# A transformer layer on one core: who turns the rotated q and k rows

## The chip, the core and the metric

One program on one core of a Trainium2 chip. The metric is device time in microseconds (us) of that core. The kernel before took 1012.53 us, the median of 3 runs (1011.42 to 1012.95).

## What is computed

A hybrid layer over 512 tokens of 1024 features, all in float32: two attention branches (a: block attention; b: attention over the 128 keys that an indexer picks), a gated merge, a mixture of 32 experts with two per token, and a gated projection. What matters here is the front of it:

```python
h = rms_norm(x, g_attn)
z = jnp.matmul(h, w_in)
qa, ka, va, qb, kb, vb, iq, ik, iw, ga, gb = jnp.split(z, offs, axis=-1)
qa, ka, qb, kb, iq = (apply_rope(heads(v), cos, sin) for v in (qa, ka, qb, kb, iq))  # 8 heads of 64
rel   = einsum('bqhd,bsd->bhqs', iq, ik) * 64 ** -0.5      # indexer, summed over heads with iw
score = einsum('bhqs,bqh->bqs', relu(rel), iw)             # causal, then the 128 largest of a row
o_a   = softmax(qa @ ka.T / 8, causal) @ va
o_b   = softmax(qb @ kb.T / 8, only the picked keys) @ vb
```

(The last lines are the reference's functions in short form. With 512 tokens the block attention's selection takes in every earlier block, so that branch a is causal attention.)

## The kernel before

Tokens lie on the 128 partitions, in four tiles of 128 (NT = 4). The matrix products `z = h @ w_in` give each of qa, ka, va, qb, kb, vb and iq as four PSUM tiles of 128 tokens by 512 columns. Weights come as **halves** of 1 MB (`HALVES`, numbered n), through a ring of four raw buffers: SP issues load n when VectorE has finished the low part of half n - 3 (`load`, L610). ScalarE rounds a half to its high part (`split_high`, L562), VectorE subtracts that from the raw weight (`split_low`, L569), and TensorE takes three products a pair (`three`, L744). Both splits run two halves ahead of the product. A half costs TensorE 48 matmuls.

ScalarE copies the finished tiles of iq, qa, ka, qb and kb, scaled, into one of two halves of `z_chunks` (`STAGE`: iq, qa, qb share one, ix, ka, kb the other), and GpSimd rotates them there in place (`rope`, L2138). A score needs q and k with the head's features on the partitions, so every rotated array has to be turned: 16 blocks of 128 by 128. In the kernel before TensorE turns them (`transposes`, L732), four to a PSUM bank, and ScalarE copies the bank to `iqt`, `qt` or `kt` (L1330): 20 groups, 80 turns and 20 copies. The next array that wants the same half of `z_chunks` waits until the groups of the one before are filled (L1342).

The order of the front is one list, `front_steps` (L118), and every engine walks it. Of weight to the change:

- `iq` is turned beside the first half of qa (`BESIDE_QA`, L219), and the eight `rel` of the second token tile, the first readers of `iqt`, are laid between the tiles of the second half of qa (`BESIDE_Z`). The `rel` of the third and fourth tile lie beside the two halves of ka.
- qa is turned behind the last `rel`, ka behind the first half of qb; VectorE runs 14 of the 16 rounds of the top-k (`topk_round`, three to a half) from the first half of qb on.
- qb and kb are turned inside the last four steps of attention a (`between` in `attention_steps`, L102), because they go to the same `qt` and `kt` that attention a reads.
- An attention is a pipeline of 16 units, (pair of heads, token tile): `scores` on TensorE (L935), scale, mask and maximum on VectorE (L1678), exponent on ScalarE (L1314), reciprocal of the sum on VectorE (L1763), the scaling of the rows on GpSimd (L2159), `turn_p` on TensorE (L947), a copy by ScalarE or VectorE, `pv` on TensorE (L962). Between attention a and b lie the two halves of vb, and the first scores of b stand between these.

Behind the front, the experts' weights (192 loads of 1 MB) go through 16 slots, most of which are regions that the front has used; SP issues each when TensorE is done with what the slot held.

Of the kernel before, what the change touches and what calls it, by code (L numbers as in the profile page):

```python
# [160 lines left out]
def place_banks():  # L161

    where, uses = {}, [0] * 8
    turns = rels = outs = 0
    for s in FRONT:
        kind = s[0]
        if kind in ("rope", "topk", "select", "merge"):
            continue
# [21 lines left out]
        elif kind == "turn" and s[1] in ("qb", "kb"):  # L190
            b = s[2] % 4
        elif kind == "turn":
            b = 4 + turns % 2
            turns += 1
# [7 lines left out]
        else:  # L202
# [102 lines left out]
def layer_kernel(nc, x, p, g_attn, w_in, w_br_a, w_br_b, w_out, g_ffn, w_grp, b_grp, w_rt, b_rt,  # L305
# [49 lines left out]
    qt = sb("qt", "qk", [P, NT, S])[:]  # L355
    kt_ = sb("kt", "qk", [P, NT, S], skip=8 * K)[:]
# [3 lines left out]
    iqt = sb("iqt", "o", [P, NT, S], skip=8 * K)[:]  # L360
# [82 lines left out]
    def turn_dst(s):  # L443
# [12 lines left out]
    def c4(name, k):  # L456
# [31 lines left out]
    ssq_done, ms_done, rms_done = (sem(n) for n in ("ssq_done", "ms_done", "rms_done"))  # L488
# [5 lines left out]
    x_squared, x_rooted, x_inv = sem("x_squared"), sem("x_rooted"), sem("x_inv")  # L494
# [110 lines left out]
    def _(sp):  # L605
# [125 lines left out]
    def _(pe):  # L731
# [140 lines left out]
        def front_step(s):  # L872
            kind, a, i = s
            if kind in ("rope", "topk", "select", "merge"):
# [40 lines left out]
            elif kind == "rel":  # L915
                t, h = a, i
                if (t, h) == (1, 0):
                    for cc in range(NT):
                        drained(pe, ("turn", "iq", cc))
# [3 lines left out]
                pe.matmul(ps[:, 0:(t + 1) * P], iqt[lo:lo + HD, h // 2, t * P:(t + 1) * P],  # L923
                          ikt[lo:lo + HD, 0:(t + 1) * P], start=True, stop=True
                          ).then_inc(bank_filled[BANK[s][0]], 1)
            elif kind == "scores":
                pair, t = unit(i)
                if i == 0:
                    for cc in range(NT):
                        drained(pe, ("turn", "q" + a, cc))  # L930
                        drained(pe, ("turn", "k" + a, cc))
                ps = [claim(pe, s + (h,)) for h in range(2)]
                for h in range(2):
                    lo = HD * h
                    pe.matmul(ps[h][:, 0:(t + 1) * P], qt[lo:lo + HD, pair, t * P:(t + 1) * P],  # L935
                              kt_[lo:lo + HD, pair, 0:(t + 1) * P], start=True, stop=True
# [352 lines left out]
    def _(act):  # L1289
        def square_x():  # L1290
# [971 lines left out]
```

## Time and profile before

The profiled execution took 1012.0 us, its span from first to last instruction is 1010.1 us, and the mean granted clock of TensorE 0.995. It lies inside the three runs (1011.42 to 1012.95).

| engine | busy us | share of the span |
|---|---|---|
| TensorE matmul | 974.6 | 96% |
| TensorE weight load | 601.6 | 60% |
| VectorE | 382.4 | 38% |
| ScalarE | 311.5 | 31% |
| GpSimd | 144.3 | 14% |

The chain that ended last is 80% TensorE and 12% DMA; of the latter nearly all (11%) is the load of the experts' `up` weights. The shares of VectorE, ScalarE and GpSimd are means over stages: the front (up to about 330 us here) holds most of the work of VectorE and GpSimd, so a stretch has to be read by itself.

### The profile page before, as it was taken

To read this page: it belongs to the slowest core of one execution; us is meant where nothing else is said; L and a number is where in the kernel's file an instruction comes from. 1 tells how busy PE (TensorE), PEld (TensorE's weight loads), DVE (VectorE), ACT (ScalarE), POOL (GpSimd) and SP (SyncE) were. 2 spreads that over 40 slices of the span, in tenths; PEclk is the share of its full clock that TensorE was granted. 3 is DMA by queue.
4 is the path that set the end of the run, shared out by engine and by line. 5 is a ranking of instruction groups with operands and counts; after the bars stand their busy time and mean duration, and the time that the engine had idled before them with its cause. 6 is when DMAs were issued, how large, how long until landed. Compare 5 with 4: busy or idle time off the path is not lost.

```text
span 1010.1 us, 12215 instructions
## 1 busy us (share of the span) xinstructions
PE 974.6 (96%) x4872; PEld 601.6 (60%) x4872; DVE 382.4 (38%) x788; ACT 311.5 (31%) x542; POOL 144.3 (14%) x141
## 2 busy tenths in 40 slices
PE   8999999999999999999999999999988998999896
PEld 6776887686788888885443444444433443343686
DVE  4344896655353436226121111111101111023875
ACT  6444334746442224242111111111110111211665
POOL 0320134926500000000000100000000000001300
PEclk9999999999999999999999999999999999999999
DMA  9512220000072350856999999999999999999701
GB/s 334 175 50 76 84 85 7 2 1 2 1 292 84 111 181 1 333 201 261 414 395 422 420 421 420 420 421 420 421 422 420 421 421 416 420 420 375 287 21 64
DMA packets 59146, 256.07 MB, mean 254 GB/s; under 512 B 12222, under 2 KB 12862, under 8 KB 34000
## 3 DMA queue, kind: packets, MB, share of 16 engines
q1 hardware_dynamic: 50224, 248.26, 61.5%
q0 software_dynamic: 2560, 4.20, 1.1%
q10 hardware_dynamic: 6304, 2.80, 1.0%
q8 instruction: 40, 0.66, 0.3%
q14 instruction: 18, 0.15, 0.0%
HBM read 248.95 MB, written 10.49 MB: 257 GB/s over the span
## 4 chain that ended last, share of the span: by engine, by line
PE 80%; DMA 12%; DVE 4%; POOL 2%; ACT 2%; issue 1%; SPq 1%; DVEq 0%
PE psum L747 37%; PE psum L1117 17%; DMA slot<-in_w_up 11%; PE psum L1073 5%; PE psum L1137 4%; PE psum L1138 4%; PE psum L1155 1%; PE psum L1093 1%; PE psum L1083 1%; PE psum L962 1%; PE psum L947 1%; DVE ple_gate_lo L1969 1%; PE psum L935 1%; PE psum L923 1%; POOL raw L2159 1%; PE psum L735 1%
## 5 line engine op out<-in xcount | busy, mean ns | idle before, releaser
L1117 PE MATMUL psum<-slot,xt 128*64 128x512 f32 x512 | 234.4, 601 | 11.6 <-DMA slot<-in_w_up 11.0
L1118 PE MATMUL psum<-slot,xt 128*64 128x512 f32 x512 | 234.7, 601 | 0.0
L1117 PEld LDWEIGHTS psum<-slot,xt 128*64 128x64 f32 x512 | 66.0, 137 | 134.6 <-issue 130.4
L2175 POOL DMA_INDIRECT pair_rows<-y,slot_pair x30 | 31.2, 1040 | 621.0 <-ACT y L1483 621.0
L1137 PE MATMUL psum<-slot,ht 128*64 128x512 f32 x256 | 115.9, 595 | 1.2 <-DVE ht L1993 1.2
L1138 PE MATMUL psum<-slot,ht 128*64 128x512 f32 x256 | 115.9, 595 | 0.0
L747 PE MATMUL psum<-w_hi,act_hi 128*128 128x512 f32 x288 | 115.4, 401 | 0.3 <-DVE act_lo L1629 0.3
L747 PE MATMUL psum<-w_lo,act_hi 128*128 128x512 f32 x288 | 112.5, 391 | 0.0
L747 PE MATMUL psum<-w_hi,act_lo 128*128 128x512 f32 x288 | 112.1, 389 | 0.0
L1476 ACT ACTIVATE small<-psum,slot_inv 64x512 f32<-64x512 f32 x32 | 21.9, 684 | 253.2 <-PE psum L1118 252.1
L572 DVE TENSOR_TENSOR w_lo<-raw,w_hi 128x2048 fp32r<-128x2048 f32 (+1 forms) x30 | 68.2, 2274 | 83.7 <-ACT w_hi L567 83.6
L567 ACT CAST w_hi<-raw 128x2048 fp32r<-128x2048 f32 (+1 forms) x30 | 55.9, 1865 | 72.1 <-PE psum L747 66.1
L1986 DVE SCALAR_TENSOR_TENSOR small<-psum,slot_inv,small 64x512 f32<-64x512 f32 x32 | 23.8, 744 | 129.2 <-ACT small L1476 129.2
L1993 DVE COPY ht<-psum 128x256 f32<-128x256 f32 x32 | 13.6, 424 | 145.3 <-PE psum L1093 142.8
L1118 PEld LDWEIGHTS psum<-slot,xt 128*64 128x64 f32 x512 | 65.9, 137 | 0.0
L747 PEld LDWEIGHTS psum<-w_hi,act_hi 128*128 128x128 f32 x288 | 54.1, 188 | 17.2 <-issue 5.9
L747 PEld LDWEIGHTS psum<-w_lo,act_hi 128*128 128x128 f32 x288 | 54.1, 188 | 11.7
L747 PEld LDWEIGHTS psum<-w_hi,act_lo 128*128 128x128 f32 x288 | 54.2, 188 | 10.4
L1942 DVE TENSOR_TENSOR xt<-psum,g_by_place 128x512 f32<-128x512 f32 x32 | 20.7, 687 | 103.1 <-PE psum L1083 103.1
L1138 PEld LDWEIGHTS psum<-slot,ht 128*64 128x64 f32 x256 | 33.7, 137 | 36.5 <-issue 36.5
L1137 PEld LDWEIGHTS psum<-slot,ht 128*64 128x64 f32 x256 | 33.7, 137 | 34.2 <-issue 32.9
L747 PE MATMUL psum<-act_hi,w_hi 128*128 128x512 f32 (+1 forms) x136 | 53.5, 394 | 0.0
(292 smaller groups left out, 1528.3 us busy)
## 6 DMA issues: line engine op xcount, KB each, us to landing
slot<-in_w_gate SPq DMA_DIRECT2D x64, 1024.0 KB, 20.7
slot<-in_w_up SPq DMA_DIRECT2D x64, 1024.0 KB, 22.2
slot<-in_w_down SPq DMA_DIRECT2D x64, 1024.0 KB, 22.2
raw<-in_w_in SPq DMA_DIRECT2D x21, 1024.0 KB, 5.0
raw<-in_w_out SPq DMA_DIRECT2D x4, 1024.0 KB, 5.4
pair_in<-pair_rows SPq DMA_DIRECT2D x4, 1024.0 KB, 14.3
slot<-in_w_ple_gate SPq DMA_DIRECT2D x4, 1024.0 KB, 8.3
rows_tok<-in_x SPq DMA_DIRECT2D x8, 256.0 KB, 5.4
```

Of the source, the lines that this page charges most:

```text
L567: act.copy(w_hi_at[n][:, 0:w], raw_at[n][:, 0:w]).then_inc(hi_done, 1)
L572: dve.tensor_tensor(w_lo_at[n][:, 0:w], raw_at[n][:, 0:w], w_hi_at[n][:, 0:w].bitcast(F32), ALU.subtract).then_inc(lo_done, 1)
L747: mms = [pe.matmul(ps, a, b, start=first and n == 0, stop=last and n == 2) for n, (a, b) in enumerate(ops)]
L1073: mm = pe.matmul(bank[(1, 7)[h]], pick[:, t, :], by_chunk(part[:, t], h), start=part is x1_hi and t == 0, stop=part is x1_lo and t == NT - 1)
L1117: mm_g = pe.matmul(ps[FIRST:2 * FIRST, :], left, g[:, k, :], start=first, stop=last)
L1118: mm_u = pe.matmul(ps[0:FIRST, :], left, u[:, k, :], start=first, stop=last)
L1137: pe.matmul(ps[0:FIRST, :], left, w[:, k, 0:512], start=first, stop=last)
L1138: mm = pe.matmul(ps[FIRST:2 * FIRST, :], left, w[:, k, 512:1024], start=first, stop=last)
L1476: act.activation(small[0:FIRST, 0, :], bank[2 + e % 2][FIRST:2 * FIRST, :], ACT.Silu, scale=slot_inv[FIRST:2 * FIRST, e:e + 1]).then_inc(s ...
L1942: dve.tensor_tensor(xt[:, q % 2, 4 * g:4 * g + 4, :], bank[g].rearrange("p (k s) -> p k s", k=4), g_by_place[:, 4 * g:4 * g + 4].unsqueeze ...
L1986: dve.scalar_tensor_tensor(out=small[0:FIRST, 1, :], in0=bank[2 + e % 2][0:FIRST, :], scalar=slot_inv[0:FIRST, e:e + 1], in1=small[0:FIRST ...
L2175: pool.indirect_dma_start(out=pairs_d.rearrange("r (h d) -> (r h) d", h=2), out_offset=bass.IndirectOffsetOnAxis(ap=index, axis=0), in_=y, ...
```

## The change

VectorE turns each 128 by 512 tile of `z_chunks` in place, in blocks of 32 by 32 (new step `flip`, four instructions for an array). Within a block rows and columns are then exchanged, but the blocks themselves still stand where they stood. SP moves these: for each pair of a source quarter and a destination quarter of the partitions one DMA, 16 DMAs for an array (`flip_blocks`), each of 32 partitions by 16 blocks by 32 elements, so 512 pieces of 128 bytes and 64 KB. For this `iqt`, `qt` and `kt` are laid out by token tile first. The 80 turns on TensorE and the 20 copies on ScalarE are gone. The readers wait on a new semaphore `flipped`.

Where SP issues them is set by a table, behind the loads n = 9, 12, 14 and 16. Some semaphores are merged, to make room for the two new ones; the instructions around them stay.

```diff
-def attention_steps(branch, between=()):
+def attention_steps(branch):
...
-        if u >= NU - 1:
-            out += between[:2]
-            between = between[2:]
...
+    flip = lambda name: [("flip", name, 0)]
-    st += z("qa")[:1] + [("ix_back", 0, 0), ("rope", "ix", 0)] + turn("iq", NT) + turn("ix", 1)
+    st += z("qa")[:1] + [("ix_back", 0, 0), ("rope", "ix", 0)] + flip("iq") + turn("ix", 1)
...
-    st += z("ka")[:1] + rel(2) + z("ka")[1:] + rel(3) + [("rope", "ka", 0)] + turn("qa", NT)
+    st += z("ka")[:1] + rel(2) + flip("qa") + z("ka")[1:] + rel(3) + [("rope", "ka", 0)]
...
-        if n == 0:
-            st += turn("ka", NT)
+        st += {0: flip("ka"), 3: flip("qb"), 4: flip("kb")}.get(n, [])
...
-    st += [("scores", "a", 2)] + attention_steps("a", turn("qb", NT) + turn("kb", NT))
+    st += [("scores", "a", 2)] + attention_steps("a")
...
-BESIDE_QA = {0: [("ix_back", 0, 0)], 1: [("turn", "iq", 0), ("turn", "iq", 1)], 2: [("turn", "iq", 2), ("turn", "iq", 3)],
-             3: [("turn", "ix", 0)]}
+BESIDE_QA = {0: [("ix_back", 0, 0)], 1: [], 2: [], 3: [("turn", "ix", 0)]}
+FLIPS = ["iq", "qa", "ka", "qb", "kb"]
+FLIP_BEHIND_LOAD = {9: ["iq"], 12: ["qa"], 14: ["ka"], 16: ["qb", "kb"]}
+QUARTER = P // 4
...
+    def flip_done(eng, name):
+
+        eng.wait_ge(flipped, 16 * 16 * (FLIPS.index(name) + 1))
...
+        def flip_blocks(name):
+
+            n = FLIPS.index(name)
+            sp.wait_ge(flip_ready, n + 1)
+            if n and name != "kb":
+                sp.wait_ge(flipped, 16 * 16 * n)
+            if name == "qb":
+                for h in range(2):
+                    filled(sp, ("scores", "a", NU - 1, h))
+            dst = {"iq": iqt, "qa": qt, "qb": qt, "ka": kt_, "kb": kt_}[name]
+            z = stage_z[:, STAGE[name]].rearrange("p t (c b j) -> p (t c) b j", b=4, j=QUARTER)
+            to = dst.rearrange("p t c (a j) -> p (t c) a j", a=4, j=QUARTER)
+            for a in range(4):
+                for b in range(4):
+                    sp.dma_start(to[QUARTER * b:QUARTER * b + QUARTER, :, a, :], z[QUARTER * a:QUARTER * a + QUARTER, :, b, :]
+                                 ).then_inc(flipped, 16)
...
+            for name in FLIP_BEHIND_LOAD.get(n, []):
+                flip_blocks(name)
...
                 if (t, h) == (1, 0):
-                    for cc in range(NT):
-                        drained(pe, ("turn", "iq", cc))
+                    flip_done(pe, "iq")
                     drained(pe, ("turn", "ix", 0))
...
                 if i == 0:
-                    for cc in range(NT):
-                        drained(pe, ("turn", "q" + a, cc))
-                        drained(pe, ("turn", "k" + a, cc))
+                    flip_done(pe, "k" + a)
...
                     prev = ROPES[ROPES.index(a) - 2]
-                    for cc in range(1 if prev == "ix" else NT):
-                        filled(act, ("turn", prev, cc))
+                    if prev == "ix":
+                        filled(act, ("turn", prev, 0))
+                    else:
+                        flip_done(act, prev)
...
+            if kind == "flip":
+                dve.wait_ge(roped, ROPES.index(a) + 1)
+                z = stage_z[:, STAGE[a]]
+                for t in range(NT):
+                    ins = dve.transpose(z[:, t], z[:, t])
+                ins.then_inc(flip_ready, 1)
+                return
```

The order of instructions on SP, from load n = 2 on. `raw` is the ring of weight halves, `x6` six instructions in a row of that form.

```order
L617 DMA raw<-in_w_in 128x8x72 [waits front_loaded_2]
L617 DMA raw<-in_w_in 128x4x512 [waits front_loaded_3]
L617 DMA raw<-in_w_in 128x4x512 [waits lo_done] x13
L617 DMA raw<-in_w_br_a 128x4x512 [waits bank_filled_7,lo_done]
L617 DMA raw<-in_w_in 128x4x512 [waits bank_filled_7,lo_done]
```

That was the kernel before: loads n = 2, 3, the thirteen from 4 to 16, and the next two. The changed kernel, from behind load n = 9:

```order
L645 DMA iqt<-z_chunks 32x16x32 [waits flip_ready]
L645 DMA iqt<-z_chunks 32x16x32 x15
L615 DMA raw<-in_w_in 128x4x512 [waits lo_done] x3
L645 DMA qt<-z_chunks 32x16x32 [waits flipped,flip_ready]
L645 DMA qt<-z_chunks 32x16x32 x15
L615 DMA raw<-in_w_in 128x4x512 [waits lo_done] x2
L645 DMA kt<-z_chunks 32x16x32 [waits flipped,flip_ready]
L645 DMA kt<-z_chunks 32x16x32 x15
L615 DMA raw<-in_w_in 128x4x512 [waits lo_done] x2
L645 DMA qt<-z_chunks 32x16x32 [waits bank_filled_2,bank_filled_3,flipped,flip_ready]
L645 DMA qt<-z_chunks 32x16x32 x15
L645 DMA kt<-z_chunks 32x16x32 [waits flip_ready]
```

Eighty DMAs now stand among the loads; those of qb and kb wait for the last scores of attention a (`bank_filled_2` and `bank_filled_3`), and the loads behind them stand behind that wait.

On TensorE, the last half of qa up to its first `rel` (L923 before, L939 now): before

```order
L747 MATMUL psum<-w_hi,act_hi 128x512
L747 MATMUL psum<-w_hi,act_lo 128x512
L747 MATMUL psum<-w_lo,act_hi 128x512
L923 MATMUL psum<-ikt,iqt 128x256 [waits bank_drained_5,bank_drained_4,bank_drained_6]
L923 MATMUL psum<-ikt,iqt 128x256 [waits bank_drained_7]
```

and now

```order
L764 MATMUL psum<-w_hi,act_hi 128x512
L764 MATMUL psum<-w_hi,act_lo 128x512
L764 MATMUL psum<-w_lo,act_hi 128x512
L939 MATMUL psum<-ikt,iqt 128x256 [waits bank_drained_6,bank_drained_4,flipped]
L939 MATMUL psum<-ikt,iqt 128x256 [waits bank_drained_7]
```

The place is the same; the 16 turns of iq, eight of them 36 and eight 24 weight matmuls ahead of it, are gone, and the first `rel` waits for the DMAs instead of ScalarE's copies.

On VectorE, between the third and the fourth top-k round (L1772 and L1775 before, L1795 and L1798 now): before

```order
L1775 MATCH_REPLACE work<-m_137,work 128x384 [waits max_done]
L1775 MATCH_REPLACE work<-m_137,work 128x512 [waits max_done]
L572 TENSOR_TENSOR w_lo<-raw,w_hi 128x2048 [waits hi_done]
L1772 MAX m_137<-work 128x8 [waits mark_done] x3
L1775 MATCH_REPLACE work<-m_137,work 128x256 [waits max_done]
```

and now

```order
L1798 MATCH_REPLACE work<-m_137,work 128x384 [waits max_done]
L1798 MATCH_REPLACE work<-m_137,work 128x512 [waits max_done]
L1639 STREAM_TRANSPOSE z_chunks<-z_chunks 128x512 [waits roped]
L1639 STREAM_TRANSPOSE z_chunks<-z_chunks 128x512 x3
L570 TENSOR_TENSOR w_lo<-raw,w_hi 128x2048 [waits hi_done]
L1795 MAX m_137<-work 128x8 [waits mark_done] x3
```

The four block turns of ka stand ahead of the low part of the next half; those of qb and kb stand in the same way behind the twelfth and the fourteenth round.

## Rows read from the trace of the kernel before

**Rows 1.** Windows: us, busy (x) of PE, PEld, DVE, ACT, POOL, clock, DMA share, GB/s.
```profile
140.00:155.00 15.00, 15.00 (x68) 12.42 (x67) 15.00 (x33) 5.84 (x6) 5.23 (x5) 1.00 0.36 82
...
180.00:200.00 20.00, 18.97 (x170) 11.74 (x168) 13.27 (x51) 14.17 (x44) 18.90 (x18) 1.00 0.01 2
```

**Rows 2.** Timeline of PE near 46: start us, us, engine, operation [idle before <-releaser].
```profile
46.55 1.03 PE L735 MATMUL psum<-cst,z_chunks 128*128 128x128 f32 x8
...
47.34 0.47 PE L747 MATMUL psum<-w_hi,act_hi 128*128 128x512 f32 x1
...
57.12 0.70 PE L923 MATMUL psum<-ikt,iqt 64*128 64x256 f32 x4
```

**Rows 3.** Timeline of DVE near 46.
```profile
46.25 0.18 DVE L1655 SCALAR_TENSOR_TENSOR iws<-psum,inv_x 128x32 f32<-128x32 f32 x1
56.91 2.29 DVE L572 TENSOR_TENSOR w_lo<-raw,w_hi 128x2048 fp32r<-128x2048 f32 x1 [10.47 <-ACT w_hi L567]
```

**Rows 4.** Timeline of DVE inside the top-k rounds.
```profile
125.88 0.68 DVE L1775 MATCH_REPLACE8 work<-m,work 128x512 f32<-128x512 f32 x1
126.48 1.47 DVE L1772 MAX8 m<-work 128x8 f32<-128x256 f32 x3
```

**Rows 5.** Timeline of SP, back-to-back issues, from its second row on.
```profile
4.98 2.14 SPq L635 DMA_DIRECT2D rows_tok<-in_x  x4
```

**Rows 6.** DMA issues: KB each, median us from issue to landing.
```profile
cst<-constants SPq DMA_DIRECT2D x1, 64.0 KB, 2.0
```

**Rows 7.** Instructions of tile wr: ns of one (min, median, max).
```profile
L1401 ACTq DMA_DIRECT2D wr<-in_w_rt x1: 604/604/604, 150.2 to 150.2; - x1
```

**Rows 8.** DMA queue of ACT, 150 to 155: packets, MB, share of 16 engines.
```profile
q10 hardware_dynamic: 3536, 0.17, 44.3%
```

**Rows 9.** Timeline of DVE, from the last rel to the third score tile.
```profile
100.58 2.40 DVE L1670 SCALAR_TENSOR_TENSOR work<-small,iws,work 128x512 f32<-128x512 f32 x2 [2.42 <-ACT small L1372]
...
105.18 2.29 DVE L572 TENSOR_TENSOR w_lo<-raw,w_hi 128x2048 fp32r<-128x2048 f32 x1 [2.20 <-ACT w_hi L567]
...
118.34 2.29 DVE L572 TENSOR_TENSOR w_lo<-raw,w_hi 128x2048 fp32r<-128x2048 f32 x1 [1.98 <-ACT w_hi L567]
...
160.65 0.67 DVE L1678 CUSTOM_DVE_ANT_0 small<-psum,cst 128x512 f32<-128x512 f32 x1
...
165.50 2.29 DVE L572 TENSOR_TENSOR w_lo<-raw,w_hi 128x2048 fp32r<-128x2048 f32 x1 [2.41 <-ACT w_hi L567]
...
172.72 0.56 DVE L1678 CUSTOM_DVE_ANT_0 small<-psum,cst 128x384 f32<-128x384 f32 x1 [4.93 <-PE psum L935]
```

**Rows 10.** Timeline of POOL in the first attention.
```profile
173.93 3.62 POOL L2159 TENSOR_SCALAR small<-small,rs 128x128 f32<-128x128 f32 x4 [7.63 <-DVE rs L1763]
...
204.10 1.82 POOL L2159 TENSOR_SCALAR small<-small,rs 128x256 f32<-128x256 f32 x2
```

**Rows 11.** Timeline of PE: its last scores of a, and what follows.
```profile
199.41 0.70 PE L935 MATMUL psum<-kt,qt 64*128 64x256 f32 x4
...
209.36 0.66 PE L962 MATMUL psum<-gain,v 128*64 128x128 f32 x8
...
209.95 0.50 PE L747 MATMUL psum<-w_hi,act_hi 128*128 128x512 f32 x1
...
221.05 1.35 PE L935 MATMUL psum<-kt,qt 64*128 64x512 f32 x8
```

**Rows 12.** Timeline of PE: two of its longest waits.
```profile
780.04 0.61 PE L1117 MATMUL psum<-slot,xt 128*64 128x512 f32 x1 [2.47 <-DMA slot<-in_w_up]
...
958.97 0.76 PE L747 MATMUL psum<-ple_gate_hi,tail_hi 128*128 128x512 f32 x1 [3.76 <-DVE ple_gate_lo L1969]
```

**Rows 13.** Windows of two us behind the first of them.
```profile
780.00:782.00 2.00, 1.96 (x8) 0.87 (x10) 0.00 (x0) 0.00 (x0) 0.00 (x0) 0.72 1.03 430
782.00:784.00 2.00, 2.00 (x8) 0.72 (x6) 0.00 (x0) 0.00 (x0) 0.00 (x0) 0.50 0.97 406
```

**Rows 14.** Waits of SP: engine, line, for whom: us in total, times, longest.
```profile
SPq L698 <- PE psum L1118: 164.8, 55, 14.5
```

More of the change, by code:

```diff
@@ L99, in unit @@
     return u // NT, (3, 0, 2, 1)[u % NT]
-def attention_steps(branch, between=()):
-    out, between = [], list(between)
+def attention_steps(branch):
+    out = []
     for u in range(LAG, NU + LAG + 1):
@@ L111, in attention_steps @@
             out.append(("pv", branch, u - LAG - 1))
-        if u >= NU - 1:
-            out += between[:2]
-            between = between[2:]
-    assert not between
     return out
@@ L163, in place_banks @@
     where, uses = {}, [0] * 8
-    turns = rels = outs = 0
+    rels = 0
     for s in FRONT:
         kind = s[0]
-        if kind in ("rope", "topk", "select", "merge"):
+        if kind in ("rope", "topk", "select", "merge", "flip"):
             continue
@@ L189, in place_banks @@
             b = s[2] % 4
-        elif kind == "turn" and s[1] in ("qb", "kb"):
-            b = s[2] % 4
         elif kind == "turn":
-            b = 4 + turns % 2
-            turns += 1
+            b = 4
         elif kind == "rel":
@@ L354, in layer_kernel @@
     act_lo = sb("act_lo", "lo", [P, KD, S], F32R)
-    qt = sb("qt", "qk", [P, NT, S])[:]
-    kt_ = sb("kt", "qk", [P, NT, S], skip=8 * K)[:]
+    qt = sb("qt", "qk", [P, NT, NT, P])[:]
+    kt_ = sb("kt", "qk", [P, NT, NT, P], skip=8 * K)[:]
     v_sb = sb("v", "v", [P, NT, AW])[:]
@@ L475, in layer_kernel @@
     picked, x_gathered, x_copied, halves_made = sem("picked"), sem("x_gathered"), sem("x_copied"), sem("halves_made")
-    (tail_turned, tail_high, tail_low, tail_filled, tail_gated, tail_squared, tail_rms, tail_inv, added, last_squared,
+    (tail_turned, tail_high, tail_low, tail_filled, tail_gated, tail_squared, tail_inv, added, last_squared,
      last_ms, last_rms, last_out) = (sem(n) for n in (
-         "tail_turned", "tail_high", "tail_low", "tail_filled", "tail_gated", "tail_squared", "tail_rms", "tail_inv",
+         "tail_turned", "tail_high", "tail_low", "tail_filled", "tail_gated", "tail_squared", "tail_inv",
          "added", "last_squared", "last_ms", "last_rms", "last_out"))
@@ L487, in layer_kernel @@
     x1_turned, x1t_copied, x1t_last = sem("x1_turned"), sem("x1t_copied"), sem("x1t_last")
-    ssq_done, ms_done, rms_done = (sem(n) for n in ("ssq_done", "ms_done", "rms_done"))
+    ssq_done, ms_done, rooted = (sem(n) for n in ("ssq_done", "ms_done", "rooted"))
     logits_done, slots_spread, slots_listed = (sem(n) for n in ("logits_done", "slots_spread", "slots_listed"))
@@ L513, in layer_kernel @@
     first_turned, first_low = sem("first_turned"), sem("first_low")
+    flip_ready, flipped = sem("flip_ready"), sem("flipped")
     def claim(pe, step):
@@ L873, in front_step @@
             kind, a, i = s
-            if kind in ("rope", "topk", "select", "merge"):
+            if kind in ("rope", "topk", "select", "merge", "flip"):
                 return
@@ L934, in front_step @@
                     lo = HD * h
-                    pe.matmul(ps[h][:, 0:(t + 1) * P], qt[lo:lo + HD, pair, t * P:(t + 1) * P],
-                              kt_[lo:lo + HD, pair, 0:(t + 1) * P], start=True, stop=True
+                    pe.matmul(ps[h][:, 0:(t + 1) * P].rearrange("p (t s) -> p t s", s=P), qt[lo:lo + HD, t, pair, :],
+                              kt_[lo:lo + HD, 0:t + 1, pair, :], start=True, stop=True
                               ).then_inc(bank_filled[BANK[s + (h,)][0]], 1)
@@ L1812, in route @@
             link(dve.tensor_scalar(v, ms, 1.0 / D, EPS, ALU.mult, ALU.add))
-            dve.wait_ge(rms_done, 1)
+            dve.wait_ge(rooted, 2)
             link(dve.reciprocal(y, sq))
@@ L2099, in tail_inverse @@
             dve.wait_ge(tail_squared, t + 2)
-            inverse(*(stat[:, 4 * k + t:4 * k + t + 2] for k in range(5)), inv_tail[:, t:t + 2], (tail_rms, t // 2 + 1), tail_inv)
+            inverse(*(stat[:, 4 * k + t:4 * k + t + 2] for k in range(5)), inv_tail[:, t:t + 2], (rooted, t // 2 + 3), tail_inv)
         dve.wait_ge(proj_done, 2 * NT)
```

16 lines of the change are left out of this document (7 added, 9 removed).

## The prediction, made before the changed kernel ran

> **What bounds the kernel now.** I read the windows by stage first, then the timelines of TensorE and VectorE at each turn that goes, then what waits for what in attention a. TensorE is busy nearly throughout, and a shift of it in the front counts in full later: the experts' loads wait for TensorE to finish with a slot (55 of them for 164.8 us in all, [rows 14]), so they start earlier or later with the front, and the end moves with them. But two stretches have a second bound. From 140 to 155 VectorE is busy 15.00 of 15.00 us, and from 180 to 200 GpSimd 18.90 of 20 [rows 1]. The reader is to see that taking work from TensorE is worth its full price only outside these.
>
> **What goes.** 20 groups of four turns. A pair of groups costs TensorE 0.79 us (46.55 to 47.34, [rows 2]), ten pairs some 8 us, a little more with the waits for ScalarE's copies between groups. By itself that would be the gain. The 20 copies on ScalarE go too.
>
> **The turn of iq.** Before, the first `rel` starts at 57.12 [rows 2]; two pairs less bring TensorE there at 57.12 - 1.6 = 55.5. What it now waits for: VectorE is free at 46.25 + 0.18 = 46.4 and idle for the next 10.47 us [rows 3], so its four block turns are hidden there. Their price the trace does not show. The nearest is the pass of 512 columns that is followed after 0.60 us (125.88 to 126.48, [rows 4]); I take 0.60 each, 2.4 us an array, with bounds of half and twice that. Ready at about 48.9. Then SP issues 16 DMAs. Four of 256 KB in a row take SP 2.14 us, 0.53 each [rows 5]; ScalarE's issue of 1024 small pieces took 0.60 [rows 7]; a DMA of 64 KB lands 2.0 us after its issue [rows 6]. With 0.53 the last is issued at 48.9 + 15 x 0.53 = 56.9 and lands at 58.9. The pieces are only 128 bytes. 3536 small ones took 44.3% of 16 engines over 5 us, 35.4 us, that is 10.0 ns each [rows 8]; 512 per engine make 5.1 us an array, below the 8.5 us of the issues, so I let the issue set the pace. Low end 0.32 us a DMA (5.1 / 16), high end 2.0 us (no DMA overlaps the next).
>
> So `rel` starts at 58.9 and not 57.12: plus 1.7, and TensorE has stood idle 3.3 us. In the kernel before, a wait of 3.76 us was one of its longest, and one of 2.47 us [rows 12] was followed by a granted clock of 0.72 and 0.50 over four us, so partly at 1.2 instead of 2.4 GHz: 2 x 0.28 + 2 x 0.50 = 1.6 us of full-speed work lost [rows 13]. 3.3 lies above that wait, and I count the fall: plus 1.6. Behind the wait on SP stand the loads from n = 10 on; the low part of half 10 is made at 118.34 only [rows 9]. ScalarE's first copy of qa waits for the same DMAs, beside TensorE.
>
> The Trainium skill, TensorE: Matmul & The Clock Gate, section HAM oscillation, describes just this: DMA waits between matmuls drop the clock and the next matmuls run cold. The trace agrees, with 0.50 behind the wait of 2.47 us.
>
> All later times leave out this shift of 3.3 against the kernel before; it is added at the end.
>
> **VectorE until attention a.** The turn of qa lies in front of the low part of a half that is wanted two halves later, and costs nothing. From the last `rel` on VectorE is the clock. Before, it ends these at 100.58 + 2.40 = 102.98 and then waits 2.20 us for ScalarE, which is still copying turned qa; now it goes on at 102.98: minus 2.2. The turn of ka adds 2.4, of which 1.98 us fills the wait at 118.34: the chain now stands at minus 2.2 + 2.4 - 2.0 = -1.8. The turns of qb and kb add 4.8: the scores of a, begun at 160.65, begin at 163.7. TensorE is there over 3 us earlier than before (four pairs at 0.79 for qa and ka, and the waits between them) and does the second half of va meanwhile. Behind the scores stand ScalarE's exponents and cast and then the low part at 165.50 + 3.0 = 168.5, which ends at 170.8. Before, VectorE was idle 4.93 us here, for TensorE, until 172.72 [rows 9]; now TensorE is early and 170.8 decides. GpSimd, the busiest engine of attention a, restarts at 173.93 - 1.9 = 172.0 [rows 10]. Of TensorE's gain 1.9 us is left there.
>
> **The tail of attention a.** GpSimd works without a gap until 204.10 + 1.82 = 205.9, now 204.0 [rows 10]. Before, TensorE still had turns of kb to do and began vb at 209.95. Now only the last turns (0.4, half a pair), one copy (about 0.7) and the last `pv` (0.66, [rows 11]) stand behind GpSimd: 1.8 us, so vb begins at 205.8: 4.1 or 4.2 early.
>
> **The turns of qb and kb.** SP issues 32 DMAs once the last scores of a are made: 199.41 + 0.70 - 1.9 = 198.2. Last issue 31 x 0.53 = 16.4 later, landed at 216.6. The scores of b are wanted at 205.8 + (221.05 - 209.95) = 216.9 [rows 11]. Hidden, with 0.3 us to spare: from 0.54 us a DMA on, each further 0.01 us costs 0.3. No load is held up: the next one waited until the end of attention b before.
>
> **Sum.** -4.2 (start of vb) + 1.7 (iq late) + 1.6 (clock) + 0 (kb) = -0.9 us. Against the profiled 1012.0 that is 1011.1; the median of the runs is 0.5 higher: 1012.53 - 0.9 = 1011.6.
>
> **Rivals.** *Short wait.* With 0.43 us a DMA the iq blocks land at 48.9 + 6.5 + 2.0 = 57.4, plus 0.2 instead of 1.7, TensorE is idle 1.9 us and the clock holds: -4.2 + 0.2 = -4.0, 1008.6. For it: the pieces of the last DMA alone need 0.32 us, and [rows 13] stands behind a longer wait. Against: 0.53 is the measured pace of back-to-back issues, and load 9 is in flight at the same time.
>
> *Slow pieces (slower).* If a piece from one partition quarter to another costs an engine 20 ns instead of 10.0, a DMA takes 32 x 20 = 0.64 us and the pieces set the pace. iq lands at 48.9 + 9.6 + 2.0 = 60.5, plus 3.4, with the clock 5.0; qb and kb land at 198.2 + 19.8 + 2.0 = 220.0, 3.1 behind the need: -4.2 + 5.0 + 3.1 = +3.9, 1016.4. At 1 us a DMA it would be +8.8 + 1.6 + 14.3 - 4.2 = +20.5. It decides from about 0.56 us a DMA on. For it: each DMA reads only 32 partitions and writes only 32, which no row shows; [rows 8] reads memory and writes all 128. Against: only the rate of [rows 8].
>
> The Trainium skill speaks on both sides. DMA: Bandwidth & Descriptors, section Specifications, wants 512 bytes for line rate and says that shorter ones are read, modified and written; by that this rival holds. The same page, section Why small descriptors are slow (HBM only), exempts transfers between SBUF and SBUF; by that the sum above holds. No run so far shows such a transfer.
>
> *Dear block turns.* At twice the price, iq is 2.4 later and the chain into attention a 7.2: -0.9 + 9.6 = +8.7, 1021.2; at half, minus 1.2 and minus up to 3.6: 1006.8. Nothing in the trace speaks for either.
>
> *Full price.* If VectorE is not what attention a waits for, all eight pairs behind iq count: -6.3 + 3.3 = -3.0, 1009.5. Against it stands the full window of VectorE in [rows 1].
>
> **Chances.** Forecast 0.35, its own range 1009.6 to 1013.2; short wait 0.26; slow pieces 0.27; dear (or cheap) turns 0.08; full price 0.04. The range is 1007.5 to 1021: it takes in both rivals and leaves out the far ends. A difference below 0.2%, 2.0 us, can hardly be told from none here. Faster by more: 0.07 of the forecast, 0.24 of the short wait, 0.06 of the last two, 0.37. Slower by more: 0.25 of the slow pieces, 0.05 of dear turns, 0.02 of the forecast, 0.32. The rest, 0.31, is the same.
>
> **What the next profile shows.** Block turns of 0.6 us starting at about 46.4. SP's 16 issues in 8.5 us and the last landing near 58.9; an idle stretch of TensorE of 3.3 us in front of the first `rel` (L939) and a clock under 1.00 behind it. VectorE's first score tile of a about 3 us later than 160.65 plus the shift, GpSimd's restart 1.9 us earlier than 173.93 plus the shift, vb begun at 205.8 plus the shift. No wait for DMAs in front of the first scores of b. A long wait there makes the prediction wrong towards slower; no idle time in front of the first `rel` makes it wrong towards faster.

## The result and the profile after

The changed kernel takes 1020.67 us (median of 4 runs, 1019.63 to 1021.6) against 1012.11 us (4 runs) of the kernel before: ratio 1.0084, 95% interval 1.0066 to 1.0101. It is slower by 8.6 us. The prediction said 1011.6, no change or slightly faster; the time lies just inside its range, close to the upper end. The profiled span is 1019.6 us against 1010.1, so the trace has 9.5 us to explain. Executions of one kernel scatter by 2 to 3 us, so a difference of less than about 1 us between two medians says little here.

Two new waits for DMAs stand in it. First TensorE, in the timeline around the first `rel` (start us, us, engine, operation, idle time before and what ended it):

```profile
55.27 0.39 PE L764 MATMUL psum<-w_lo,act_hi 128*128 128x512 f32 x1
61.76 1.23 PE L939 MATMUL psum<-ikt,iqt 64*128 64x256 f32 x4 [6.11 <-DMA iqt<-z_chunks]
```

TensorE is ready at 55.65, where the prediction had it, and stands still for 6.11 us. The `rel` that began at 57.12 [rows 2] begins at 61.76: plus 4.64, not 1.7. On VectorE the block turns of iq lie in the idle time of [rows 3], each four of them 2.4 to 2.5 us:

```profile
46.66 2.48 DVE L1639 STREAM_TRANSPOSE z_chunks<-z_chunks 128x512 f32<-128x512 f32 x4
55.35 2.29 DVE L570 TENSOR_TENSOR w_lo<-raw,w_hi 128x2048 fp32r<-128x2048 f32 x1 [6.21 <-ACT w_hi L565]
```

So the pieces start on time. What is late is the row of issues on SP (timeline of SP; the row's duration covers all its issues):

```profile
49.16 10.85 SPq L645 DMA_DIRECT2D iqt<-z_chunks  x16
...
204.45 11.76 SPq L645 DMA_DIRECT2D qt<-z_chunks  x16
216.25 10.74 SPq L645 DMA_DIRECT2D kt<-z_chunks  x16
```

and, one by one, ns of an issue (min, median, max), first and last start in us:

```profile
L645 SPq DMA_DIRECT2D qt<-z_chunks x32: 597/632/1723, 96.9 to 215.6; - x32
L645 SPq DMA_DIRECT2D kt<-z_chunks x32: 590/631/1612, 125.8 to 226.4; - x32
L645 SPq DMA_DIRECT2D iqt<-z_chunks x16: 617/631/755, 49.2 to 59.4; - x16
```

Sixteen take 10.85 us where [rows 5] let me expect 8.5; from start to start that is (59.4 - 49.2) / 15 = 0.68 us. (The longest of an issue, 1.6 to 1.7 us, fall in the sets of qa, ka and qb.) The granted clock behind both waits (windows of 2 us, columns as in [rows 1]):

```profile
60.00:62.00 2.00, 0.24 (x2) 0.24 (x4) 0.00 (x0) 0.26 (x1) 0.00 (x0) 0.50 0.74 92
62.00:64.00 2.00, 2.00 (x7) 1.16 (x8) 0.48 (x1) 1.09 (x3) 0.00 (x0) 0.50 0.94 314
64.00:66.00 2.00, 2.00 (x8) 1.62 (x7) 0.48 (x1) 0.00 (x0) 0.00 (x0) 0.74 0.47 183
228.00:230.00 2.00, 1.30 (x4) 0.79 (x6) 0.00 (x0) 0.00 (x0) 0.00 (x0) 0.50 0.11 15
230.00:232.00 2.00, 2.00 (x8) 1.17 (x7) 1.08 (x3) 0.35 (x1) 0.00 (x0) 0.50 0.00 0
232.00:234.00 2.00, 2.00 (x9) 1.61 (x9) 0.82 (x7) 2.00 (x9) 0.54 (x1) 0.93 0.03 8
```

A clock of 0.50 is 1.2 GHz instead of 2.4. From 61.76 to 66 it costs 2.24 x 0.50 + 2 x 0.26 = 1.6 us; behind the second wait, from 228.70, 3.3 x 0.50 and 0.1 in the next window, 1.8 us. VectorE, the answer to [rows 9]:

```profile
106.69 2.44 DVE L1693 SCALAR_TENSOR_TENSOR work<-small,iws,work 128x512 f32<-128x512 f32 x2 [2.41 <-ACT small L1388]
109.05 2.82 DVE L570 TENSOR_TENSOR w_lo<-raw,w_hi 128x2048 fp32r<-128x2048 f32 x1
...
123.08 2.24 DVE L570 TENSOR_TENSOR w_lo<-raw,w_hi 128x2048 fp32r<-128x2048 f32 x1
...
169.20 0.66 DVE L1701 CUSTOM_DVE_ANT_0 small<-psum,cst 128x512 f32<-128x512 f32 x1
...
176.25 0.55 DVE L1701 CUSTOM_DVE_ANT_0 small<-psum,cst 128x384 f32<-128x384 f32 x1
```

Against [rows 9], VectorE's part of the last `rel` is 6.1 late; the wait of 2.20 us behind it is gone (109.05 is only 3.9 late); the wait at 118.34 has been filled by the turn of ka; the scores of a are 8.5 late; and at 176.25 VectorE comes without idle time, where it idled 4.93 us before. That is the chain of the prediction, step by step; the sizes are compared further below. GpSimd [rows 10] and TensorE [rows 11]:

```profile
177.45 3.63 POOL L2182 TENSOR_SCALAR small<-small,rs 128x128 f32<-128x128 f32 x4 [2.60 <-DVE rs L1786]
...
208.30 1.83 POOL L2182 TENSOR_SCALAR small<-small,rs 128x256 f32<-128x256 f32 x2
```

```profile
211.31 0.66 PE L976 MATMUL psum<-gain,v 128*64 128x128 f32 x8
...
228.70 2.50 PE L949 MATMUL psum<-kt,qt 64*128 64x512 f32 x8 [5.61 <-DMA kt<-z_chunks]
```

The last product of attention a was over at about 210.0 and is over at 211.97; the scores of b are wanted at 228.70 - 5.61 = 223.09 and start at 228.70. From measured times alone: the scores of b are wanted 2.04 later than in the kernel before (223.09 against 221.05), wait 5.61 and lose 1.8 to the clock, together +9.45; the spans differ by 9.5. The 2.04 are the lateness of iq and its clock, 4.64 + 1.6, less 4.2 gained in between, which is the prediction's own step for vb (-4.1 or -4.2).

### The profile page after: what moved, and what is told of

The parts are those of the page before. It is cut to its first block, busy times and chain, and to the rows that moved or that the text cites. A ratio compares the mean times of both kernels' runs of the same rounds, so it can differ in the third digit from the quotient of the medians.

```text
span 1019.6 us, 12121 instructions
## 1 busy us (share of the span) xinstructions
PE 970.3 (95%) x4792; PEld 596.6 (59%) x4792; DVE 394.3 (39%) x808; ACT 301.0 (30%) x522; POOL 142.5 (14%) x141
## 4 chain that ended last, share of the span: by engine, by line
PE 70%; DMA 12%; DVE 10%; SPq 3%; ACT 2%; issue 1%; POOL 1%; DVEq 0%
PE psum L764 28%; PE psum L1131 17%; DMA slot<-in_w_up 11%; PE psum L1087 5%; PE psum L1151 4%; PE psum L1152 4%; SPq L645 3%; DVE work L1798 2%; DVE m L1795 2%; PE psum L1107 1%; PE psum L1169 1%; DVE w_lo L570 1%; PE psum L1097 1%; PE psum L949 1%; PE psum L976 1%
## 5 line engine op out<-in xcount | busy, mean ns | idle before, releaser
L1131 PE MATMUL psum<-slot,xt 128*64 128x512 f32 x512 | 232.7, 597 | 12.4 <-DMA slot<-in_w_up 11.8
L764 PEld LDWEIGHTS psum<-w_lo,act_hi 128*128 128x128 f32 x288 | 54.6, 190 | 11.8
```

The source lines that it names most:

```text
L764: mms = [pe.matmul(ps, a, b, start=first and n == 0, stop=last and n == 2) for n, (a, b) in enumerate(ops)]
L1131: mm_g = pe.matmul(ps[FIRST:2 * FIRST, :], left, g[:, k, :], start=first, stop=last)
```

## The experiments

Two theories on the pace. *Issue theory*: a DMA costs its issuing engine some 0.7 us, whatever it carries. *Piece theory*: the 16 DMA engines are held up by 128-byte pieces. Independently of both, each wait should have a price of its own. "Before" is timed in the same calls (medians 1011.87 to 1012.09).

One caution on times of day in different traces. Four of the kernels below have the same steps as the kernel before up to the first `rel`, and no DMA wait there; it starts at 57.14, 56.77, 57.59 and 55.88, and at 57.12 in the kernel before. So a later time is best counted from the first `rel` of its own trace, or the scatter of the start is taken for an effect.

**One wait removed: iq on TensorE again.**

```
-    st += ... + flip("iq") + turn("ix", 1)
+    st += ... + turn("iq", NT) + turn("ix", 1)
-BESIDE_QA = {..., 1: [], 2: [], ...}
+BESIDE_QA = {..., 1: [("turn", "iq", 0), ("turn", "iq", 1)], 2: [("turn", "iq", 2), ("turn", "iq", 3)], ...}
```

> One part undone: iq is turned by TensorE again, the other four arrays as in the changed kernel. If each DMA wait costs what stands late behind it (my theory: two separate prices, 6.1 us for iq and 7.3 for qb and kb), 6.1 comes back: 1020.7 - 6.1 = 1014.6 us, no idle stretch in front of the first rel, and still 5 to 6 us idle in front of the first scores of b. Rival (the waits hide one another, since the later one only absorbs the lateness of the first): the wait in front of the scores of b grows by what iq gave back, and the time stays near 1020.7.

Measured 1014.99 us (6 runs), ratio to before 1.0033 (1.0021 to 1.0046): 5.7 us came back of the expected 6.1. `rel` begins at 57.14 without a wait, and the wait for kb is still there:

```profile
222.85 2.50 PE L954 MATMUL psum<-kt,qt 64*128 64x512 f32 x8 [5.23 <-DMA kt<-z_chunks]
```

The rival falls: the waits don't hide one another, since SP starts the second set of DMAs behind the scores of a and so is earlier by what TensorE is.

**The other wait removed: qb and kb in two halves.** The order of a staged array is changed to head pair, token tile, column, so that a half is one run of pieces (the edit in short form):

```
+for half in range(2):
+    sp.wait_ge(flipped, ...)                         # what was issued before has landed
+    filled(sp, ("scores", "a", (NU // 2 if half == 0 else NU) - 1, h))
+    ... 32 DMAs: dst[:, 2 * half:2 * half + 2] <- z[:, 2 * half:2 * half + 2]
-scores of b, step 0: wait for kb
+scores of b, step 0: wait for the first half; step 2: wait for the second
```

> iq as in the changed kernel. qb and kb go in two halves (head pairs 0 and 1, then 2 and 3), 32 DMAs of 256 pieces each; the first half as soon as attention a has made its scores of pair 1, the second behind the last scores of a; the third scores step of b waits for the second half. Issue theory (a DMA costs SP some 0.72 us whatever its size): 23 us a half, the first lands near 210, the second near 230, before TensorE wants it near 234; no idle in front of the scores of b, 1020.7 - 7.3 = 1013.4 us. Piece theory (the pace is that of the pieces): a half takes 11.5 us, the time is the same 1013.4, but SP's pitch is about 0.36 us. So the time tests the price of the wait, and the pitch tells the two theories apart.

Measured 1014.47 us (5 runs), 1.0029 (1.0016 to 1.0043). TensorE goes into the scores of b at 224.46 without a wait, so the price of this wait is confirmed in form; 6.2 us came back of the expected 7.3. In the profiled execution the clock stayed low longer behind a wait for iq of the same length (TensorE, then windows):

```profile
61.33 1.22 PE L954 MATMUL psum<-ikt,iqt 64*128 64x256 f32 x4 [6.09 <-DMA iqt<-z_chunks]
```
```profile
64.00:66.00 2.00, 2.00 (x6) 1.58 (x5) 0.07 (x1) 0.00 (x0) 0.00 (x0) 0.50 0.21 82
66.00:68.00 2.00, 2.00 (x7) 1.27 (x7) 0.00 (x0) 0.17 (x1) 0.00 (x0) 0.64 0.00 0
```

The clock is 0.50 from 60 to 66 there: 4.67 x 0.50 + 2 x 0.36 = 3.1 us lost and not 1.6. The pace of SP, one by one:

```profile
L643 SPq DMA_DIRECT2D qt<-z_chunks x32: 585/611/1269, 187.6 to 221.6; - x32
```

256 pieces take 611 ns to issue, 512 took 631: the pace does not follow the pieces. This is the first blow to the piece theory.

**Both waits removed.** The two edits together.

> Both of the above: iq on TensorE, qa and ka as in the changed kernel, qb and kb in halves. By the sum of the prediction without its two DMA waits the start of vb is 4.2 us earlier than before and nothing waits behind it: 1012.1 - 4.2 = 1007.9 us; the two prices read from the trace of the changed kernel give 1020.7 - 6.1 - 7.3 = 1007.3. Rival (VectorE, which makes the block turns, is the bound and gives nothing back): 1012.1, no faster than before.

Measured 1007.86 us (5 runs), ratio 0.9963 (0.9949 to 0.9978): faster than the kernel before. Attention a's last product ends at 206.1 against 210.0, 3.9 early, or 3.6 counted from the first `rel` (56.77 against 57.12), where 4.2 were predicted; nothing is lost behind it. GpSimd, then TensorE:

```profile
170.98 3.62 POOL L2205 TENSOR_SCALAR small<-small,rs 128x128 f32<-128x128 f32 x4 [2.61 <-DVE rs L1809]
...
202.42 1.82 POOL L2205 TENSOR_SCALAR small<-small,rs 128x256 f32<-128x256 f32 x2
```
```profile
205.43 0.66 PE L998 MATMUL psum<-gain,v 128*64 128x128 f32 x8
217.13 1.35 PE L971 MATMUL psum<-kt,qt 64*128 64x512 f32 x8
```

**Two queues for iq.** Half of the 16 DMAs are issued by ScalarE:

```
-                for b in range(4):
+                for b in range(0, 4, 2 if name == "iq" else 1):      # SP; ScalarE issues b = 1 and 3
```

> Only who issues the 16 DMAs of iq is changed: 8 from SP and 8 from ScalarE. Issue theory: 8 x 0.72 us on either side, the last issue near 54 and landed near 56.5, TensorE idle below 1 us and no fall of the clock: 1020.7 - 6.1 = 1014.6 us. Piece theory (16 engines work off the pieces at the measured pace): the blocks land near 61.7 as before, 1020.7 us.

Measured 1019.79 us (4 runs), 1.0080 (1.0065 to 1.0095). The time is what the piece theory expected; but the timeline of ScalarE shows that the trial was badly built. Its eight issues stand behind its copy of ix, start at 53.12 and end at 58.8, when SP has been done since 54.85. `rel` waits until 60.48. It tells nothing apart, so I moved them:

```
+            if s == ("flip", "iq", 0):
+                act.wait_ge(flip_ready, 1)           # in front of the copy of ix
```

> As the previous kernel with two queues, but ScalarE issues its 8 DMAs of iq as soon as the block turns are made (near 49) instead of behind its copy of ix (53.1). Issue theory: both queues at 0.7 us a DMA side by side, last issue near 54.6, landed near 57, rel there and not at 61.8, TensorE idle about 1.3 us, clock held: 1020.7 - 4.7 - 1.5 = 1014.5 us. Piece theory: side by side each queue falls to about 1.4 us a DMA, rel stays near 61.7, 1020.7 us.

Measured 1019.23 us (4 runs), 1.0071 (1.0049 to 1.0093). Now both queues run at once (timelines of SP, ScalarE and TensorE):

```profile
48.19 6.75 SPq L645 DMA_DIRECT2D iqt<-z_chunks  x8
```
```profile
48.19 6.85 ACTq L1341 DMA_DIRECT2D iqt<-z_chunks  x8
```
```profile
58.00 0.70 PE L939 MATMUL psum<-ikt,iqt 64*128 64x256 f32 x4 [3.33 <-DMA iqt<-z_chunks]
```

Sixteen in 6.85 us and not in 10.85: the wait falls from 6.11 to 3.33. Neither theory had its number. Two queues do share the work, so SP's issuing was what set the pace; but side by side an issue takes 0.84 to 0.86 us, and landing 3.5 to 3.7 us instead of 2.3, so a second bound stands close behind, and this run doesn't say which. The Trainium skill, DMA: Bandwidth & Descriptors, section Issuing engines are not separate DMA queues, says that a second issuing engine saves only issue time, "which is usually small relative to the DMA itself". The first half agrees with the trace. The second fits one of these DMAs (issued in 0.63 us, landed in 2.3) but not the set: 16 issues one behind the other take 10.85 us, most of the time until the last has landed. I had expected 6.2 us back and got 1.4 by the median of four runs (1017.39 to 1020.21). The trace explains about 2.2: the wait for iq is 2.8 shorter and the one for kb 0.55 longer (6.16), and the clock fell all the same, though only after TensorE had resumed at 58.00:

```profile
58.00:60.00 2.00, 2.00 (x9) 1.44 (x10) 2.00 (x2) 1.33 (x3) 0.00 (x0) 0.87 0.00 0
60.00:62.00 2.00, 2.00 (x7) 1.51 (x6) 0.67 (x2) 0.00 (x0) 0.00 (x0) 0.50 0.53 87
```

**TensorE kept busy in the wait for iq.**

```
+                    for _ in range(24):
+                        pe.matmul(ps, act_hi[:, 0, 0:P], act_hi[:, 1, :], start=True, stop=True)
                     flip_done(pe, "iq")
```

> The changed kernel; in front of its wait for the blocks of iq TensorE makes 24 products of act_hi with itself (128x512, about 5.5 us), whose result nobody reads. The wait stays. If the granted clock of 0.62 to 0.68 behind the wait is what idling costs: clock 1.00 behind it, 1.5 us less up to the last rel, 1020.7 - 1.5 = 1019.2 us. Rival (the clock falls for another reason, or the time is lost in the DMA wait alone): no change.

Measured 1019.12 us (6 runs), 1.0067 (1.0049 to 1.0084), about 1.5 us less than the changed kernel, though the intervals of the two overlap. The trace is clearer: idle time 0.67 us, and no fall:

```profile
61.19 0.70 PE L943 MATMUL psum<-ikt,iqt 64*128 64x256 f32 x4 [0.67 <-DMA iqt<-z_chunks]
```
```profile
62.00:64.00 2.00, 2.00 (x10) 1.62 (x11) 0.97 (x2) 0.58 (x2) 0.00 (x0) 1.00 1.01 386
```

**The pace by size of the pieces.** Other data, same bytes and same count (the blocks land in wrong places, so the total time means nothing here; the edit in short form):

```
+if name in ("iq", "kb"):   to4[32 rows, :, a, :] <- z4[32 rows, :, b, :]      # 128 pieces of 512 bytes
+if name == "qa":           dst[:, a, b, :] <- z4[:, a, b, :]                   # 128 partitions, 512 bytes each
```

> A measurement of SP's pace by form, each DMA of 64 KB; the blocks land in wrong places, so this is for the issue times and not for the total. iq and kb: 32 partitions, 128 pieces of 512 bytes in place of 512 of 128. qa: all 128 partitions, one piece of 512 bytes each. ka and qb as in the changed kernel (512 pieces of 128 bytes). Issue theory: all five near 0.7 us a DMA, rel near 61.8. Piece theory: 0.7 us for ka and qb, clearly below (0.2 to 0.5) for the long pieces, and rel earlier by 15 times the difference.

One run, read only for the issues (ns of one, min, median, max):

```profile
L654 SPq DMA_DIRECT2D qt<-z_chunks x16: 550/602/735, 96.9 to 106.8; - x16
```
```profile
L647 SPq DMA_DIRECT2D iqt<-z_chunks x16: 588/601/755, 48.4 to 58.2; - x16
```

A quarter of the pieces at four times the length takes 0.601 us where the short ones took 0.631, and 128 partitions instead of 32 the same. Landing goes from 2.3 to 2.0 us. The piece theory falls as an explanation of the 16 DMAs on one queue. The rule of the Trainium skill that the prediction had on its own side (DMA: Bandwidth & Descriptors, section Why small descriptors are slow (HBM only): transfers within SBUF are exempt) agrees with this run, where short pieces cost 0.03 us an issue and 0.3 us of landing.

**The pace by source.** But why 0.63 and not the 0.53 of [rows 5]? Those rows read HBM.

```
+if name == "iq":   to[32 rows, :, a, :] <- w_in[32 rows, 0:2048] as (n b j), [:, :, b, :]     # 512 pieces, from HBM
+if name == "qa":   dst[:, a, b, :] <- w_in rows, 128 columns                                 # 128 pieces, from HBM
```

> A measurement of SP's pace by source; the blocks hold other data, so this is for the issue times and not for the total. iq: 16 DMAs with the shape of the change (32 partitions, 512 pieces of 128 bytes) but from w_in in HBM. qa: 16 DMAs of 64 KB, 128 partitions, one piece of 512 bytes each, from HBM. ka, qb, kb as in the changed kernel. If reading from SBUF is what makes an issue dear: 0.5 us a DMA for iq and qa, as for the loads of x, and 0.7 for ka. If it is the write into SBUF or the mere DMA of 64 KB: 0.65 to 0.7 for all.

One run, again for the issues:

```profile
L653 SPq DMA_DIRECT2D iqt<-in_w_in x16: 337/488/494, 48.8 to 56.6; - x16
L653 SPq DMA_DIRECT2D kt<-z_chunks x16: 627/631/642, 213.9 to 224.0; - x16
```
```profile
L648 SPq DMA_DIRECT2D qt<-in_w_in x16: 427/432/655, 95.3 to 102.7; - x16
```

The very shape of the change, read from HBM, goes at (56.6 - 48.8) / 15 = 0.52 us a DMA, the 0.53 of the prediction; read from SBUF, kb in the same run goes at (224.0 - 213.9) / 15 = 0.67, and iq in the changed kernel at 0.68. With 128 partitions and 512-byte pieces it is (102.7 - 95.3) / 15 = 0.49 from HBM against 0.66 from SBUF in the run by size of the pieces. The dear thing is an issue whose source is SBUF. (The landing goes the other way: 2.7 us for iq from HBM, 2.3 from SBUF.) Why an issue costs more stays open.

**Twelve DMAs instead of sixteen.** The blocks that stay in their own quarter of the partitions, four DMAs of the 16, are not moved by DMA. For iq VectorE copies them; for qb and kb they are left out, so that attention b computes with old blocks there.

```
+                    if a == b and name not in ("qa", "ka"):
+                        continue
+# iq only: four copies on VectorE, iqt[own, :, :, own] <- z[own][..., own]
```

> 12 DMAs instead of 16 for iq, qb and kb: the blocks on the diagonal don't go by DMA. Those of iq are copied by the idle VectorE; those of qb and kb are left out (they hold the blocks of qa and ka). At the measured 0.72 us a DMA twelve take about what sixteen take at the 0.53 of the prediction, so this puts the prediction's own numbers to the test: iq lands at 49 + 11 x 0.72 + 2.3 = 59.2, TensorE idle 3.5 us, the clock falls and costs 1.5; vb begins at 209.95 - 4.2 + 3.5 = 209.3; qb and kb land at 201.8 + 23 x 0.72 + 2.3 = 220.7 against a need of 220.4: 1011.9 - 4.2 + 3.5 + 0.3 = 1011.5 us. If the price of a DMA wait isn't what its lateness says: clearly above, toward 1020.

Measured 1009.92 us (10 runs), 0.9977 (0.9965 to 0.9989). The issues of an array now take 8.2 us, nearly the 8.5 of the prediction, and the trace is nearly the one predicted: `rel` at 58.23, idle 3.36 (predicted 58.9 and 3.3), no wait in front of the scores of b.

```profile
58.23 0.70 PE L942 MATMUL psum<-ikt,iqt 64*128 64x256 f32 x4 [3.36 <-DMA iqt<-z_chunks]
...
217.98 1.35 PE L952 MATMUL psum<-kt,qt 64*128 64x512 f32 x8
```

What does not come behind the wait for iq is the fall of the clock:

```profile
60.00:62.00 2.00, 2.00 (x11) 1.39 (x11) 0.46 (x1) 0.07 (x1) 0.00 (x0) 1.00 0.75 284
```

It held at 2.4 GHz behind 3.36 us of idling, while in the run with two queues it fell to 1.2 behind 3.33 us, and in [rows 12, 13] behind 2.47. That fits the time, 1.6 below the expected 1011.5. But this is one execution, and the clock is not always so kind in it: behind a later wait, for an expert's `up` weights, it falls.

```profile
832.59 1.09 PE L1134 MATMUL psum<-slot,xt 128*64 128x512 f32 x1 [3.14 <-DMA slot<-in_w_up]
```
```profile
834.00:836.00 2.00, 2.00 (x6) 0.53 (x4) 0.00 (x0) 0.00 (x0) 0.00 (x0) 0.50 1.00 414
```

Eight of the traces have such a wait between 830 and 844: the clock fell behind 2.44, 2.81, 3.12 and twice 3.14 us and held behind 1.79, 2.25 and 2.69. The edits do not touch that stretch. It is a likely part of the scatter of 2 to 3 us, though no run shows how much.

**Only qa and ka.** iq, qb and kb are turned by TensorE.

```
-        st += {0: flip("ka"), 3: flip("qb"), 4: flip("kb")}.get(n, [])
+        st += {0: flip("ka")}.get(n, [])
-    ... attention_steps("a")
+    ... attention_steps("a", turn("qb", NT) + turn("kb", NT))
```

> Only qa and ka are turned in the new way; iq, qb and kb are turned by TensorE as before. This asks who bounds the way into attention a. If VectorE does (the prediction): its 4.8 us of block turns for qb and kb go, so attention a starts where TensorE's four pairs less let it, 3.2 us before the kernel before and not 2.9 as in the kernel with both waits removed (about the same), but the eight pairs of turns stand behind attention a again: vb starts about 4.1 us behind GpSimd's end instead of 1.8, so at 209.95 - 3.1 = 206.9 and the time is 1012.0 - 3.1 = 1008.9 us. Rival (TensorE's work is worth its full price everywhere): four of eight pairs are given back, half of the gain of 4.0 us is left, 1010.0 us.

Measured 1007.39 us (5 runs), 0.9954 (0.9940 to 0.9967), the fastest of all, if not clearly faster than the 1007.86 of both waits removed. GpSimd restarts at

```profile
169.52 3.62 POOL L2199 TENSOR_SCALAR small<-small,rs 128x128 f32<-128x128 f32 x4 [5.10 <-DVE rs L1803]
```

4.4 us before [rows 10] and 1.5 before the 170.98 of the kernel with both waits removed (counted from the first `rel`, here at 57.59: 4.9 and 2.3), and attention a ends as much earlier than before, with the turns of qb and kb behind it. The rival's 1010.0 falls; my 1008.9 was a little high, since TensorE, which decides here, makes its third score step at 167.35 and not at 171.77: the four pairs were worth 4.4 us (4.9 from the first `rel`), with the waits between them, and not 3.2. That TensorE decides is seen on VectorE:

```profile
168.30 0.56 DVE L1718 CUSTOM_DVE_ANT_0 small<-psum,cst 128x384 f32<-128x384 f32 x1 [2.40 <-PE psum L965]
```

**More work on VectorE.** The kernel with both waits removed, with eight more block turns:

```
+                if a in ("qb", "kb"):
+                    for t in range(NT):
+                        dve.transpose(iqt[:, t], z[:, t])
```

> The kernel with both waits removed, with eight more block turns on VectorE (four beside those of qb, four beside those of kb, into a buffer that is free then), 4.8 us of work that nobody reads. If VectorE is what attention a waits for, as the prediction has it: GpSimd's restart and the start of vb come 4.8 us later, 1007.9 + 4.8 = 1012.7 us. Rival (VectorE has slack there, TensorE decides): no change, 1007.9.

Measured 1012.14 us (10 runs), 0.9996 (0.9986 to 1.0005), 4.3 above 1007.86.

```profile
174.81 3.62 POOL L2208 TENSOR_SCALAR small<-small,rs 128x128 f32<-128x128 f32 x4 [2.60 <-DVE rs L1812]
```
```profile
210.03 0.66 PE L998 MATMUL psum<-gain,v 128*64 128x128 f32 x8
```

GpSimd restarts 3.8 later than at 170.98. But this trace starts early, with its first `rel` at 55.88 and not 56.77; counted from there it is 4.7 of the 4.8 us added. So up to attention a VectorE's work counts at full price. The last product, at 210.03 against 205.43, is 4.6 later, 5.5 from the first `rel`: another 0.8 is lost inside attention a, where GpSimd waits 3.0 us for VectorE in all, against 2.2 without the added turns.

## Why the prediction was wrong

*What failed* is one number in the step of iq, used again in the step of qb and kb: "Four of 256 KB in a row take SP 2.14 us, 0.53 each". The pace was taken from DMAs that read HBM and used for DMAs that read SBUF. Measured is 0.67 to 0.68 for iq and kb (10.85 and 10.74 us for 16) and 0.74 to 0.78 for qb, qa and ka (11.8 to 12.5). The same shape from HBM goes at 0.52. With 0.68 in the prediction's own formula iq lands at 49.2 + 15 x 0.68 + 2.3 = 61.7, measured 61.76; and the text had said that from 0.54 us on each 0.01 us of pace costs 0.3 in front of the scores of b: (0.71 - 0.54) x 31 = 5.3, measured 5.61 (0.71 is the mean pace of the 32, (226.4 - 204.45) / 31, and they landed in 2.3 and not 2.0 us). One error, 0.15 us an issue in the first place and 0.18 in the second, was paid over 15 and over 31 steps, and in the second it brought a fall of the clock that the sum did not have.

*Slow pieces*, the rival on the slower side, gave 1016.4 at 0.64 us a DMA. Its form was right (both waits, in these places) and its cause wrong: 128-byte pieces against 512-byte ones change an issue by 0.03 us. Its price was low mainly because it left out the clock behind the second wait (1.8 us) and took 0.64 where 0.68 and 0.71 were measured.

*Short wait* took 0.43 us a DMA: no set from SBUF comes near it; the nearest is the 0.49 of 128 pieces from HBM.

*The block turns* at 0.60 each: right, 2.47 us an array. *Their start* at 46.4: 46.66. *The landing* at 2.0 us: 2.3.

*The clock* (+1.6): right in size in the changed kernel, where it fell behind 6.11 us, and tied to the idling by the filled wait: in the four traces in which TensorE idled 4.65 to 6.11 us there the clock fell, with the wait filled it did not. (One trace stands on that side, and the time moved by 1.5 us with overlapping intervals.) But the text treated 3.3 us of idling as enough, and the run with twelve DMAs idled 3.36 us without a fall. The length of the idling alone does not decide at this size, nor does it set how long the clock stays low (1.6 us lost behind 6.11 us, 3.1 behind 6.09), and that step was told with more certainty than [rows 12, 13] give.

*The chain of VectorE* (-2.2, +2.4, -2.0, +4.8): right in its steps; the *shift of 3.3* was 4.64 + 1.6, some 6.3 with the waits as they were. Scores of a predicted at 163.7 + 6.3 = 170.0, measured 169.20; GpSimd's restart at 172.0 + 6.3 = 178.3, measured 177.45. That VectorE decides there is shown by the 4.8 us of added work, of which 4.7 arrive at GpSimd's restart.

*Start of vb* (-4.2): in the changed kernel 1.95 late against 2.1 (6.3 - 4.2) by the prediction; with both waits removed -3.9, -3.6 from the first `rel`. Two errors cancel in part here, and that is luck. GpSimd restarts earlier than forecast (with both waits removed 2.6 early from the first `rel`, not 1.9), but it is done at 202.42 + 1.82 = 204.24, only 1.3 early: inside attention a it waits 2.2 us in all for VectorE, 1.1 before, while the prediction let it work "without a gap". The tail behind it is as forecast (1.8).

*qb and kb* (0, "0.3 us to spare"): SP started at 204.45, predicted 198.2 + 6.3 = 204.5, and the need came at 223.1, predicted 216.9 + 6.3 = 223.2. Only the 16.4 us up to the last issue were 21.95. A spare of 0.3 us on a chain of 31 steps should not have been a zero in the sum: an error of 2% in the step eats it.

*Full price* for TensorE's turns was given 0.04. It fails in the changed kernel. But only because the same change puts 4.8 us on VectorE: with qa and ka alone the stretch becomes TensorE's again, and it gains 4.4, against 3.9 with VectorE's turns of qb and kb.

## What to carry to other kernels

When a step is cut into many DMAs of one queue, the issues are the transfer: take the time of an issue from a row with the same source memory and multiply it by their number before looking at bytes. Move such a step only where its consumer is further away than that product (here qa and ka, with tens of microseconds), and leave it on the compute engine where the consumer is next in line; the part of the change that obeys this gives 4.6 us, the whole loses 8.6. And what is handed to an idle engine is free only in its idle time: here qb and kb turned by VectorE bring no more (1007.86) than turned by TensorE (1007.39).

## What the runs showed of the hardware

- An issue on SP takes 0.60 to 0.63 us when the source is SBUF and 0.43 to 0.49 us when it is HBM, for the same 64 KB; four times fewer pieces save 0.03 us, and 128 partitions instead of 32 nothing. The same shape lands 2.3 us after its issue from SBUF and 2.7 from HBM.
- Two queues issuing at once took 0.84 to 0.86 us an issue each, against 0.68 alone, and landing 3.5 to 3.7 us against 2.3; the set of 16 still took 6.85 us of issues and not 10.85.
- Two waits of nearly the same length behind nearly the same work (3.33 and 3.36 us of idling) left the clock at 1.2 GHz in one run and at 2.4 GHz in the other, and two of 6.11 and 6.09 us cost 1.6 and 3.1 us of full-speed work.
